# Seven block products for pairs of gate/up chunks in the FFNs of a two-block network

## The reference

```
def swiglu(h, w_gate, w_up, w_down):          # w_gate, w_up: 1024 x 2816, w_down: 2816 x 1024
    return (jax.nn.silu(h @ w_gate) * (h @ w_up)) @ w_down
x = x + 0.5 * swiglu(rmsnorm(x, g), w_gate, w_up, w_down)
```

## Time and profile before

| | us |
|---|---|
| median of 3 runs | 2638.79 (2638.25 to 2642.26) |
| span of the profiled execution | 2636.4 |
| TensorE busy (16746 matmuls) | 2616.3 |
| VectorE busy | 1497.4 |
| ScalarE busy | 1435.8 |
| GpSimd busy | 851.6 |

### The profile page before, as it was taken

The page is one execution under the profiler, slowest core; times in us unless marked ns, Lnnn a source line. Parts: engine busy times, 40 slices in busy tenths (PEclk is TensorE's granted clock), DMA queues, the critical chain, the costliest instruction groups (busy, mean ns, idle before and its releaser), DMA issues.

```text
span 2636.4 us, 45280 instructions
## 1 busy us (share of the span) xinstructions
PE 2616.3 (99%) x16746; PEld 2280.3 (86%) x16746; DVE 1497.4 (57%) x2457; ACT 1435.8 (54%) x2122; POOL 851.6 (32%) x443
## 2 busy tenths in 40 slices
PE   9999999999999999999999999999999999999999
PEld 8888998888888998888889999988888899999887
DVE  5553645545543745545556787355455567873654
ACT  5546665445445655445445645664455557456643
POOL 0007672000017675000008755810000086558100
PEclk9999999999999999999999999999999999999999
DMA  7555546655655546556557742566565587425664
GB/s 226 184 182 177 146 155 188 187 189 180 189 176 175 152 153 198 184 184 194 187 164 184 170 88 82 170 190 187 180 198 186 153 195 166 84 79 184 191 184 144
DMA packets 351973, 447.17 MB, mean 170 GB/s; under 512 B 32446, under 2 KB 241344, under 8 KB 351776
## 3 DMA queue, kind: packets, MB, share of 16 engines
q1 hardware_dynamic: 350032, 442.80, 56.8%
q10 hardware_dynamic: 816, 1.21, 0.1%
q0 software_dynamic: 928, 0.45, 0.1%
HBM read 443.31 MB, written 1.05 MB: 169 GB/s over the span
## 4 chain that ended last, share of the span: by engine, by line
PE 95%; ACT 3%; DVE 2%; issue 0%; POOL 0%; DVEq 0%; ACTq 0%; POOLq 0%
PE PS L522 29%; PE PS L524 29%; PE PS L523 28%; PE PS L725 1%; PE PS L1110 1%; PE PS L1183 1%; PE PS L691 1%; PE PS L1173 1%; PE PS L913 1%; DVE PS L2303 1%; PE PS L960 0%; ACT xh L1320 0%; ACT wh L547 0%; PE PS L826 0%; PE PS L1207 0%
## 5 line engine op out<-in xcount | busy, mean ns | idle before, releaser
L547 ACT ACTIVATE wh<-ring 128x1024 fp32r<-128x1024 f32 (+2 forms) x840 | 883.4, 1055 | 879.9 <-PE PS L522 857.0
L555 POOL TENSOR_TENSOR wl<-ring,wh 128x1024 fp32r<-128x1024 f32 (+2 forms) x332 | 786.1, 2384 | 1589.6 <-ACT wh L547 1589.1
L555 DVE TENSOR_TENSOR wl<-ring,wh 128x1024 fp32r<-128x1024 f32 x508 | 621.4, 1225 | 612.7 <-ACT wh L547 612.4
L522 PE MATMUL PS<-wh,xh 128*128 128x512 f32 (+2 forms) x1760 | 692.3, 393 | 1.0 <-POOL wl L555 1.0
L524 PE MATMUL PS<-wh,xl 128*128 128x512 f32 (+2 forms) x1760 | 682.5, 388 | 0.0
L523 PE MATMUL PS<-wl,xh 128*128 128x512 f32 (+2 forms) x1760 | 681.3, 387 | 0.0
L522 PE MATMUL PS<-xh,wh 128*128 128x256 f32 x1536 | 444.8, 290 | 0.1
L524 PE MATMUL PS<-xh,wl 128*128 128x256 f32 x1536 | 434.4, 283 | 0.0
L523 PE MATMUL PS<-xl,wh 128*128 128x256 f32 x1536 | 434.3, 283 | 0.0
L524 PEld LDWEIGHTS PS<-wh,xl 128*128 128x128 f32 x1760 | 330.5, 188 | 68.4
L522 PEld LDWEIGHTS PS<-wh,xh 128*128 128x128 f32 x1760 | 330.7, 188 | 68.0 <-issue 2.7
(11 more groups left out here) (319 smaller groups left out, 2439.0 us busy)
## 6 DMA issues: line engine op xcount, KB each, us to landing
ring<-in_ffn_w_in_dram SPq DMA_DIRECT2D x352, 256.0 KB, 3.0
ring<-in_mix_w_in_dram SPq DMA_DIRECT2D x256, 256.0 KB, 3.9
ring<-in_ffn_w_gate_dram SPq DMA_DIRECT2D x176, 256.0 KB, 2.9
ring<-in_ffn_w_up_dram SPq DMA_DIRECT2D x176, 256.0 KB, 3.1
ring<-in_ffn_w_down_dram SPq DMA_DIRECT2D x176, 256.0 KB, 2.8
ring<-in_w_in_dram SPq DMA_DIRECT2D x176, 256.0 KB, 3.0
ring<-in_ffn_w_out_dram SPq DMA_DIRECT2D x176, 256.0 KB, 2.8
ring<-in_w_branch_dram SPq DMA_DIRECT2D x32, 256.0 KB, 2.9
```

The source lines that it names most:

```text
L522: first_ = mm(o, w[0], x[0], start=start, stop=False, skip_group_check=True)
L547: act_(dst, src, ACT.Copy).then_inc(hi_ready, 1)
L555: (engine or v_).tensor_tensor(dst, src, part_views(t, wh)[0], ALU.subtract).then_inc(lo[t.slot()], 1)
```

## The change

In each FFN the chunks (3, 4), (7, 8) and (9, 10) become pairs. A pair's weights are four blocks b11, b12, b21, b22: rows 1 to 512 or 513 to 1024, first or second chunk, 512 columns of gate and up each, as 128x2048. The pair's results are 2x2 blocks too (token half x chunk). They are made from seven block products M1 to M7, where eight would be usual; each has four row blocks x 3 = 12 matmuls. Three products take blocks as they are (b11, b22, b21), four take differences: T1 = b12 - b11, T2 = b22 - T1, T3 = b22 - b12, T4 = b21 - T2. The activations are summed likewise, once per FFN (S0 to S4, in `sq`). Partial results are added in PSUM or by VectorE (c12, c22, c11).

VectorE makes all differences, sums and low parts. ScalarE makes the high parts of 128x2048 and copies three products out of PSUM. The low parts of blocks are written over the raw blocks in `W`, so an operation waits until the raw block has been read for the last time. The blocks don't pass the ring: SyncE loads them into `W` in two DMAs of 512 KB each; those of the next pair wait for products of the pair before. Pairs 0 and 1 stand after chunks 2 and 6; pair 2 (chunks 9 and 10) stands inside the down projection, after its eighth tile. A product's parts take one or two of the ring's four slots for parts; M6 and M2 have their low part in a slot too.

Besides: one bank for all turns where there were two; SyncE's loops are written out; the 28 loads of the second block's small parameters go from GpSimd's queue to SyncE's, in the fourth FFN, behind pair 0's loads; VectorE's wait for GpSimd's masks stands later; some scratch lies elsewhere.

The constants, SyncE's order and ScalarE's wait before a high part:

```diff
+PAIRS = ((3, 4), (7, 8), (9, 10))
+DOWN_FRONT = 8
+SUM_OF = {"M1": 0, "M5": 1, "M6": 2, "M3": 4, "M7": 5, "M2": 6, "M4": 8}
+RAW_OF = {"M1": "b11", "M5": "t1", "M6": "t2", "M3": "b22", "M7": "t3", "M2": "b21", "M4": "t4"}
+BEHIND = ("M6", "M2")
...
+            def pair_blocks(p, after=lambda i: None):
+                for i, (name, product) in enumerate((("b11", "M1"), ("b12", "M7"), ("b22", "M3"), ("b21", "M2"))):
...
+                        sp.wait_ge(track_[0].sem, track_[0].at(f"{tag_}.{product}.{p_}", lay_))
...
+                    load_block(sp, p, name, gate, up)
+                    after(i)
...
+            pair_blocks(0, lambda i: tile(2, i))
...
+            for kp in range(4):
+                tile(5, kp)
+            pair_blocks(1)
+            for kp in range(4):
+                tile(6, kp)
...
+                if c == DOWN_FRONT // 2:
+                    pair_blocks(2)
...
+        def high_sum(e, t, ff, s, tag, p, n):
+            u = SUM_OF[n]
+            sum_ready(e, ff, s, tag, p, n)
+            e.wait_ge(used, t.number(u) + 1)
```

TensorE's order, of a pair and of the FFN:

```diff
+            def two_chunks(p):
...
+                product("M1", x_part(0, 0), True)
...
+                product("M5", sum_part(1, 1), True)
+                if p < 2:
+                    turn(PAIRS[p][0] - 1)
...
+                product("M6", sum_part(0, 0))
...
+                product("M3", sum_part(1, 0))
...
+                product("M7", sum_part(0, 1))
+                product("M2", x_part(4, 0), True)
+                pe.wait_ge(ff[2].sem, ff[2].at(f"{tag}.c22.{p}"))
+                product("M4", x_part(4, 1))
...
+            plain(1, (0,))
+            plain(2, (1,))
+            two_chunks(0)
+            plain(5, (4, 3))
+            plain(6, (5,))
+            two_chunks(1)
```

VectorE's order, of a pair from M6 on and of the FFN:

```diff
+            def two_chunks(p, c, d, between=lambda: None):
+                low_behind("M6", 0)
+                low_behind("M6", 1)
+                if p < 2:
+                    gated(c - 1)
+                low_whole(p, "M3", "T3")
+                if p < 2:
+                    turned(c - 1)
+                low_whole(p, "M7", "T3")
+                low_behind("M2", 0)
+                low_behind("M2", 1)
+                summed(p, bank(7), bank(7), u2s, "M3", "u2s", "c12")
+                low_whole(p, "M4", "T4")
+                summed(p, m5s, bank(6), m5s, "M7", "m5s", "c22")
+                t.k += PAIR_SLOTS
+                gated_of(d, 0, bank(7, CHUNK, 2 * CHUNK))
+                low(e, t, 1)
...
+                turned(d)
+                low(e, t, 1)
+                between()
+                turned(c)
+            gated(0)
+            low(e, t, 3)
+            turned(0)
+            sums()
+            low(e, t, 1)
+            sums_low()
+            low(e, t, 1)
+            chunk(1)
+            gated(1)
+            low(e, t, 1)
+            turned(1)
+            block1(0)
+            low_whole(0, "M1", "T1")
+            block2(0)
+            low_whole(0, "M5", "T2")
+            block3(0)
+            block4(0)
+            chunk(2)
+            two_chunks(0, *PAIRS[0], lambda: block1(1))
+            low(e, t, 2)
+            block2(1)
+            block3(1)
+            gated(5)
...
+            low_whole(1, "M1", "T1")
+            low_whole(1, "M5", "T2")
+            block4(1)
+            two_chunks(1, *PAIRS[1], lambda: block1(2))
```

More of the change, by code:

```diff
@@ L253, in program @@
         second["ffn"] = [track(f"second_ffn_{e}") for e in ("products", "scalar", "vector")]
+        blocks_in = {n: sem(f"weight_block_loaded_{n}") for n in ("b11", "b12", "b21", "b22")}
         def bc(ap, n):
@@ L290, in view @@
             return W[:, at:at + width]
[L292 removed]
+        rows = post
+        off[0] = 14656
         srow = view(P)
@@ L370, in kmajor, with ffn_number @@
             return w2d.rearrange("(k p) n -> p k n", p=P)
-        def load_ffn(sp, t, gate, up, down, between=lambda: None):
-            def chunk(it, c0):
-                for kp in range(4):
[L376 to L380, removed]
-            between()
[L382 to L388, removed]
+        def ffn_number(s):
+            return 2 * (s // 3) + s % 3 // 2
@@ new lines, in between @@
+                    def between(last=lay == LAYERS - 1 and half == 1):
+                        if last:
+                            load_params2(sp)
+                    load_ffn(sp, t, first["ffn"], f"f{half}", lay, kmajor(a["ffn_w_gate"][lay, half]),
+                             kmajor(a["ffn_w_up"][lay, half]), a["ffn_w_down"][lay, half],
+                             (first["mix"], lay) if half == 1 else None, before, between)
+                    before = (first["ffn"], f"f{half}", lay, 2)
@@ L508, in program @@
         qd = view(512).rearrange("p (h n) -> p h n", h=4)
+        assert off[0] <= 13824, off[0]
+        off[0] = 13824
+        for c in range(QT):
+            DU["U", c] = view(512).rearrange("p (h n) -> p h n", h=4)
         wT, st = DU["T", 0], DU["T", 1]
@@ L712, in pe_xt_mix, with pe_sum_product @@
                 pe_xt(pe, s, q, sqt, lambda h: pe.wait_ge(xn_made, 4 * m + 2 * q + 1 + h))
+        def pe_sum_product(pe, t, ff, tag, p, n, part, start):
+            u = SUM_OF[n]
+            low_ready(pe, t, u)
+            if n in BEHIND:
+                low_ready(pe, t, u + 1)
+            for k in range(4):
+                at = slice(k % 2 * HALF, (k % 2 + 1) * HALF)
+                lows_ = wp[:, k // 2, t.slot(u + 1), at] if n in BEHIND else low_of[RAW_OF[n]][:, k * HALF:(k + 1) * HALF]
+                one, ins = three(bank(SUM_BANKS[n]), part(k), (wp[:, k // 2, t.slot(u), at], lows_), start and k == 0, k == 3)
+                if k == 0:
+                    one.then_inc(used, 2 if n in ("M3", "M4") else 1)
+            ins.then_inc(ff[0].sem, ff[0].did(f"{tag}.{n}.{p}"))
         def pe_ffn(pe, t, ff, s, tag, first_at, by_half=False, between=lambda: None, down_at=None, inner=lambda: None):
@@ L1451, in act_ffn @@
+            turned(5)
+            for c in range(3, 7):
+                chunk(c)
+            sums_front(1)
+            two_chunks(1, *PAIRS[1])
+            high(e, t, DOWN_FRONT - 5)
+            for c in range(7, CHUNKS + 1):
+                chunk(c)
+            sums_front(2)
+            two_chunks(2, *PAIRS[2])
             tables(LN_EXP)
-            high(e, t, 8)
+            high(e, t, 4)
             midway()
-            high(e, t, FB - AHEAD - 2 - 8 + more)
+            high(e, t, FB - DOWN_FRONT - 5 - 4 + more)
@@ new lines, in block2, with block3, block4 @@
+            def block2(p):
+                e.wait_ge(blocks_in["b22"], blocks_landed(s, p))
+                own(f"T1.{p}")
+                block(p, "t2", "b22", "t1")
+            def block3(p):
+                own(f"T2.{p}")
+                block(p, "t3", "b22", "b12")
+            def block4(p):
+                e.wait_ge(blocks_in["b21"], blocks_landed(s, p))
+                if p == 0:
+                    own("sl1")
+                else:
+                    e.wait_ge(ff[0].sem, ff[0].at(f"{tag}.M4.{p - 1}"))
+                block(p, "t4", "b21", "t2")
@@ L2040, in dve_ffn @@
+            for c in range(7, CHUNKS + 1):
+                chunk(c)
+            low_whole(2, "M1", "T1")
+            low_whole(2, "M5", "T2")
+            block4(2)
+            two_chunks(2, *PAIRS[2])
+            low(e, t, 4)
             midway()
-            low(e, t, FB - AHEAD - 2 - 8)
+            low(e, t, FB - DOWN_FRONT - 5 - 4)
         def dve_index(e, tr, j):
```

419 lines of the change are left out of this document (309 added, 110 removed).

## The result

The changed kernel takes 2750.44 us (median of 4 runs, 2749.39 to 2755.98) where the kernel before takes 2638.59: a ratio of 1.0426, 95% interval [1.0411, 1.0441], 112 us slower. The forecast was 2715, its range 2660 to 2775.

A forecast was written before the change was run, and what follows sets the result against it. TensorE, busy 99% of the span, was taken as the bound. Per FFN 8.16 us saved and 17.8 lost in waits make 9.6 more; eight FFNs add 77 to the span of 2636.4: 2713, median 2715, range 2660 to 2775.

The forecast's parts named there:

- rival 3: Clock falls to 1.2 GHz in two long waits per FFN, one product after each at half rate: 2759; chance 0.20.
- Rival 2: VectorE keeps up because 2048-wide operations are much cheaper than two of 1024: faster, 2574 if all hidden; chance 0.08.
- First step: Before chunk 1's gating VectorE also has sums and their low parts; TensorE waits 3.1 us at chunk 1's turn.
- Third: From chunk 2's turn to the sum M4 waits for: VectorE 11.4 us, TensorE 11.37, wait 0.1.
- Second step: Up to chunk 2's gating: VectorE 20.9 us, TensorE 14.1; wait 6.8, some 2 before M5, 4.7 at the turn.
- Fourth step: From M4's sum to chunk 5's gating: 2.8 us wait from VectorE's queue plus 3.5 from late loading, 6.3.
- Rival 1: Pair 1's blocks land in time, by faster transfer or shorter landing: 13.2 us lost per FFN, 2679; chance 0.18.
- Fifth step: Pair 1 itself waits 0.2 us; from pair 1 to pair 2, in the down projection, 1.3.
- The clock: Granted clock 1.00 in every stretch read; the likeliest forecast added nothing for slow matmuls after waits.

The follow-up runs named there:

- e1_fill: The changed kernel with TensorE doing useless matmuls into a spare bank before the turns of chunks 1, 2 and 5: 2724.5 us.
- e2_tiles_first: The changed kernel with chunk 6's tiles ahead of pair 1's blocks b22 and b21 in SyncE's queue: 2713.4 us.
- e4_gate_first: The changed kernel with VectorE making T2 and T3 of pair 1 behind chunk 5's gating: 2717.9 us.
- e6: The changed kernel with pair 0 undone, chunks 3 and 4 plain again, all else in its order: 2750.3 us.
- e7: As e6, with each block loaded behind one chunk's tiles, the sums over three chunks, and T2 and T3 of pair 1 earlier: 2652.0 us.

## Why the forecast came out as it did

The direction and the mechanism were right; the clock was the term that was missing from the likeliest case, and the time fell between it and the third rival (2759), outside the likeliest interval (2690 to 2735) and inside the range. e1_fill is nearly the kernel that the sum describes, with the clock at 0.999: 2724.5, for 2715.

*Prices.* A 2048-wide operation takes VectorE 2288 ns alone and about 2.2 us behind another (taken: 2.29 and 2.2), ScalarE 1915 (taken: 2020). Matmuls 16458 as counted; VectorE 1939 us (1977), ScalarE 1604 (1630). Rival 2 is out.

*First step*, 3.1 us at turn 1: 2.93. *Third*, 0.1: no listed wait.

*Second step*, 6.8: 3.98, all at the turn. From gating to gating VectorE takes 19.9 us (457.94 to 477.80) where 20.9 were taken, TensorE from turn to turn 15.9 (458.04 to 473.92) where 14.1 were, since its clock is 0.87 from 459 to 469. VectorE's wait of 2.05 us for the high part of M5 is not there, and this was a reading error in the code: M5's weights are T1 (`"M5": "t1"`), not T2. ScalarE makes their high part while VectorE makes T2, and VectorE goes on at once:

```profile
465.73 2.28 DVE L2314 TENSOR_TENSOR W<-W 128x2048 f32<-128x2048 f32 x1
468.04 2.29 DVE L690 TENSOR_TENSOR sum_lows<-W,wp 128x2048 fp32r<-128x2048 f32 x1
```

That the sum of this step comes out nearly right at full clock is in part luck. In e1_fill it is 6.2: 1.61 before M5 and 4.6 from the start of the fill (468.37) to turn 2 (472.98). The wait that was misread is missing there too, but the tile ahead of T1 is done 3.6 us after the gating (452.21 to 455.77), where 1.6 were taken.

*Fourth step*, 6.3: 5.64 (7.4 in e1_fill, from 501.85 to 509.24), and by the mechanism described. M7 of pair 0 ends near 488.2, SyncE issues b12 at 488.37, and the first tile of chunk 6 has landed at 501.36: 13.0 us, where 11.8 + 1.5 were taken. SyncE's issue of b12, ScalarE's wait for the tile, then VectorE's, with T1 to T3 and the gating behind:

```profile
488.37 0.37 SPq L429 DMA_DIRECT2D W<-in_ffn_w_gate_dram  x1
```

```profile
501.36 1.06 ACT L642 ACTIVATE wp<-ring 128x1024 fp32r<-128x1024 f32 x1 [3.61 <-DMA ring<-in_ffn_w_up_dram]
```

```profile
502.45 1.23 DVE L650 TENSOR_TENSOR wp<-ring,wp 128x1024 fp32r<-128x1024 f32 x1 [3.98 <-ACT wp L642]
503.60 2.28 DVE L2314 TENSOR_TENSOR W<-W 128x2048 f32<-128x2048 f32 x1
```

Rival 1 is out: more than 318 GB/s were moved, 352, but 3.67 MB at that rate are 10.4 us, which leaves 2.6 for the landing where 1.5 were taken. And e2_tiles_first shows the split between queue (2.6) and lateness (3.0; taken: 2.8 and 3.5).

*Fifth step*, 1.5: gaps of 0.3 to 0.5 us in the down projection, 9.3 us over the eight FFNs, 1.2 in each.

*The clock*, taken as 1.00: 0.978. The forecast gave it to a rival with two waits and 5.4 us in an FFN. In the second FFN all three waits are followed by slow stretches, the one of 2.93 us too. What the Trainium skill says (TensorE: Matmul & The Clock Gate, Part 1: The HAM clock gate) is borne out by these stretches. The price of rival 3, 44 us, lies between the 26 of e1_fill and the 50 that the clock takes from a working TensorE. But not each wait of some 3 us brings a slow stretch: the 2.96 us at turn 1 of the third FFN are the one of the 24 that does not, and in e4_gate_first five of the seven waits of 2.9 to 3.0 us at turn 1 have none before TensorE's next wait. The second FFN of e4_gate_first, behind a wait of 2.94 us that ends at 454.62:

```profile
455.00:464.00 9.00, 9.00 (x42) 7.33 (x41) 7.17 (x5) 5.28 (x4) 0.00 (x0) 1.00 0.57 175
```

So the step that was mis-sized is the clock: nought was taken, and holding the clock up gives 26 us back, 3 in an FFN; the slow stretches take 6 from TensorE's work, but hide some of the waits. That is also why only 14.9 us of waits more than before are listed in an FFN, where 17.8 were taken.

## What to carry to other kernels

A product scheme that trades TensorE's work for another engine's is worth only what that engine has free just there: count its time between two points that TensorE waits for, not over the span. Put the added sums and loads where queues have slack, well ahead of their use: with the same products, order alone was worth 98 us (e6 to e7), and two pairs placed so beat the kernel before by 0.7% where three, placed close to their use, lost 4%. Whether three pairs can be placed so was not tried. And where a busy TensorE is made to wait some 3 us or more, add to the price of each wait the slow clock that may stand behind it.

## What was not expected of the hardware

The DMA engines moved 335 to 352 GB/s over 14 us at a share of 1.02 to 1.10, above the 318 GB/s of the earlier trace rows. The Trainium skill (DMA: Bandwidth & Descriptors, Specifications) gives about 358 GB/s for one core from HBM; these stretches come close to it. A wait of 2.93 us was followed by a granted clock of 0.87 over 10 us, one of 2.94 us in e4_gate_first by 1.00 over 9 us. In the kernel before, with no wait above 1.9 us, the clock of the runs was 0.999 to 1.000.
